# A two-block transformer kernel on one core: the norms' reciprocal square root as a power on GpSimd, and large SBUF buffers at steps of 1,024 bytes

## What is computed

```python
def rmsnorm(x, g):
    return x * lax.rsqrt(jnp.mean(x * x, axis=-1, keepdims=True) + EPS) * g    # EPS = 1e-6

def first_block(x, c, ctx, c_ctx, ...):
    h  = modulate(rmsnorm(x, norm1_g), sh1, sc1)         # norm 1: 512 tokens
    hc = modulate(rmsnorm(ctx, norm1_g), csh1, csc1)     # norm 2: 256 context tokens
    x = x + g1 * merge_branches(neighborhood_attention(...), spatial_gating(...), ...) # "out"
    h2 = modulate(rmsnorm(x, norm2_g), sh2, sc2)         # norm 3
    x = x + g2 * peer_ffn(h2, ...)      # 16,384 experts, computed densely: U, gates, then V
    return rmsnorm(x, final_g)                           # norm 4

def second_block(x, ...):
    proj = rms_norm(x, norm_mix) @ w_in                  # norm 5
    x = x + (sigmoid(ga) * (att @ w_att_o) + sigmoid(gr) * (ret @ w_ret_o)) @ w_out
    h = rms_norm(x, norm_ffn)                            # norm 6
    x = x + (silu(h @ w_gate) * (h @ w_up)) @ w_down
    return rms_norm(x, final_norm)                       # norm 7
```

## Time and profile before

| | |
|---|---|
| median of 3 runs | 3146.31 us |
| profiled execution | 3148.33 us, its span 3146.5 us |
| TensorE matmul busy | 2984.7 us, 95% of the span, 13,212 instructions |
| VectorE busy | 1462.3 us, 46% |
| ScalarE busy | 1080.6 us, 34% |
| GpSimd busy | 1167.5 us, 37% |
| mean granted TensorE clock | 0.969 |
| DMA | 417.05 MB, 133 GB/s on average |

### The profile page before, as it was taken

The page is one execution under the profiler, slowest core; times in us unless marked ns, Lnnn a source line. Parts: engine busy times, 40 slices in busy tenths (PEclk is TensorE's granted clock), DMA queues, the critical chain, the costliest instruction groups (busy, mean ns, idle before and its releaser), DMA issues.

```text
span 3146.5 us, 39584 instructions
## 1 busy us (share of the span) xinstructions
PE 2984.7 (95%) x13212; PEld 2372.9 (75%) x13256; DVE 1462.3 (46%) x2578; ACT 1080.6 (34%) x1740; POOL 1167.5 (37%) x494
## 2 busy tenths in 40 slices
PE   3988999899999999999999999999798899999998
PEld 2756877688888888887888888888585588778876
DVE  8266723149964555551555555555416731221101
ACT  4244333333335555553222222222313332232221
POOL 5310534335443333334444444444240054344442
PEclk7989999999999999999999999999898899999999
DMA  5310722224454545545666666666130033223321
GB/s 224 107 41 1 278 93 94 87 94 146 150 180 146 194 161 187 186 163 201 192 187 187 189 187 187 187 187 174 53 95 25 11 107 94 87 80 100 94 94 53
DMA packets 252690, 417.05 MB, mean 133 GB/s; under 512 B 149456, under 2 KB 150864, under 8 KB 250816
## 3 DMA queue, kind: packets, MB, share of 16 engines
q1 hardware_dynamic: 227440, 371.51, 37.8%
q10 hardware_dynamic: 22976, 37.23, 3.3%
q0 software_dynamic: 2192, 7.24, 1.0%
HBM read 345.93 MB, written 69.99 MB: 132 GB/s over the span
## 4 chain that ended last, share of the span: by engine, by line
PE 91%; DVE 4%; issue 2%; ACT 1%; DMA 1%; DVEq 0%; SPq 0%; ACTq 0%
PE bank L952 27%; PE bank L954 27%; PE bank L953 27%; PE bank L1168 2%; PE bank L1157 2%; PE bank L1049 1%; PE bank L993 1%; DVE T L1374 1%; PE bank L1029 1%; DVE rr L1370 1%; PE bank L1041 1%; PE bank L1286 1%; PE bank L1268 0%; DMA act_dram<-actb 0%; PE bank L1122 0%
## 5 line engine op out<-in xcount | busy, mean ns | idle before, releaser
L500 POOL TENSOR_TENSOR wlo<-wraw,whi 128x1024 fp32r<-128x1024 f32 x456 | 1122.6, 2463 | 1753.9 <-ACT whi L580 1753.7
L952 PE MATMUL bank<-HH,whi 128*128 128x512 f32 x2160 | 872.7, 404 | 77.2 <-DVE HL L1385 50.4
L954 PE MATMUL bank<-HH,wlo 128*128 128x512 f32 x2160 | 845.5, 391 | 0.0
L953 PE MATMUL bank<-HL,whi 128*128 128x512 f32 x2160 | 844.3, 391 | 0.0
L580 ACT ACTIVATE whi<-wraw 128x1024 fp32r<-128x1024 f32 x456 | 482.1, 1057 | 951.7 <-PE bank L954 855.0
L952 PEld LDWEIGHTS bank<-HH,whi 128*128 128x128 f32 x2160 | 408.5, 189 | 177.8 <-issue 75.6
L1683 DVE TENSOR_TENSOR WL<-AJ,WH 128x512 fp32r<-128x512 f32 x128 | 315.0, 2461 | 352.9 <-ACT WH L823 352.9
L954 PEld LDWEIGHTS bank<-HH,wlo 128*128 128x128 f32 x2160 | 407.8, 189 | 87.5
L953 PEld LDWEIGHTS bank<-HL,whi 128*128 128x128 f32 x2160 | 408.7, 189 | 84.1 <-issue 0.2
L952 PE MATMUL bank<-WH,whi 128*128 128x512 f32 x1024 | 405.8, 396 | 2.8 <-DVE WL L1683 2.8
L953 PE MATMUL bank<-WL,whi 128*128 128x512 f32 x1024 | 405.6, 396 | 0.0
(11 more groups left out here) (259 smaller groups left out, 3046.2 us busy)
## 6 DMA issues: line engine op xcount, KB each, us to landing
wraw<-in_w SPq DMA_DIRECT2D x456, 512.0 KB, 3.6
act_dram<-actb ACTq DMA_DIRECT2D x128, 256.0 KB, 2.9
gate_dram<-GS SPq DMA_DIRECT2D x8, 4096.0 KB, 13.0
AJ<-act_dram SPq DMA_DIRECT2D x128, 256.0 KB, 2.8
GJ<-gate_dram SPq DMA_DIRECT2D x128, 256.0 KB, 3.8
adaw<-in_ada SPq DMA_DIRECT2D x32, 512.0 KB, 5.4
ada<-in_ada SPq DMA_DIRECT2D x16, 512.0 KB, 14.2
E<-in_rpb POOLq DMA_DIRECT2D x16, 224.0 KB, 4.9
```

The source lines that it names most:

```text
L500: nc.gpsimd.tensor_tensor(wlo[:, slot, :, :].rearrange("p k c -> p (k c)"), wraw[:, slot, :, :].rearrange("p k c -> p (k c)"), whi[:, slot ...
L952: pe.matmul(out_, ah, bh, start=first, stop=False, **kw)
L953: pe.matmul(out_, ah, bl, start=False, stop=False, **kw)
L954: return pe.matmul(out_, al, bh, start=False, stop=last, **kw)
```

## The change

1. Each norm's square root on ScalarE (`norm_root`) goes, and so does VectorE's reciprocal. VectorE adds EPS to the sum while it copies it out of PSUM into `rms` (signal `n_var`), GpSimd raises it to the power -1/2 into `rstd` (signal `n_root`), and VectorE goes on. GpSimd's seven powers are put between its weight subtractions: the first behind its eight context products, the second behind the low parts of tiles 0 to 2, the others where the next tile waits for that norm anyway.
2. The matrix of ones becomes a matrix of 1/D (`mean`), so that the sum is a mean; the group norm's constants take the factor back.
3. The small tiles are allocated first, and tiles of 2,048 bytes or more start on a multiple of 1,024. `wraw` then starts at byte 23,552 and the phase buffers at 138,240.

```diff
@@ -104,10 +105,26 @@
-            return lambda name, shape, dt=F32: stack.enter_context(nc.sbuf_tensor(name, shape, dt))
+            def tile(name, shape, dt=F32):
+
+                big = 4 * math.prod(shape[1:]) >= 2048
+                return stack.enter_context(nc.sbuf_tensor(name, shape, dt, align_bytes=1024 if big else 32))
+            return tile
         sb = allocator(ctx)
+        cols = sb("cols", [P, NCOL])
+        mod = sb("mod", [P, 48, 2])
+        gsc = sb("gsc", [P, 3, KB])
+        ident = sb("ident", [P, P])
+        mean = sb("mean", [P, P])
+        iota = sb("iota", [P, P])
+        eps = sb("eps", [P, 2])
+        st = sb("st", [P, 24])
+        bn = sb("bn", [P, TB, 6])
+        rr = sb("rr", [P, 2, S])
+        rms, rstd = rr[:, 0, :], rr[:, 1, :]
+        sc_row = rr[:, :, :].rearrange("p a b -> p (a b)")
@@ -115,18 +132,6 @@
-        cols = sb("cols", [P, NCOL])
-        mod = sb("mod", [P, 48, 2])
-        gsc = sb("gsc", [P, 3, KB])
-        ident = sb("ident", [P, P])
-        ones = sb("ones", [P, P])
-        iota = sb("iota", [P, P])
-        eps = sb("eps", [P, 1])
-        rr = sb("rr", [P, 2, S])
-        rms, rstd = rr[:, 0, :], rr[:, 1, :]
-        sc_row = rr[:, :, :].rearrange("p a b -> p (a b)")
-        st = sb("st", [P, 24])
-        bn = sb("bn", [P, TB, 6])
@@ -294,6 +299,7 @@
+        n_var = sem("n_var")
@@ -384,7 +390,7 @@
-            for dst, src in ((X[:, :, :], A["x"]), (cols[:, :], A["cols"]), (ones[:, :], A["ones"])):
+            for dst, src in ((X[:, :, :], A["x"]), (cols[:, :], A["cols"]), (mean[:, :], A["mean"])):
@@ -516,10 +522,21 @@
+            pool.wait_ge(n_eps, 2)
+            norms = [0]
+
+            def norm_rstd(width):
+
+                norms[0] += 1
+                pool.wait_ge(n_var, norms[0])
+                nc.gpsimd.tensor_tensor(rstd[:, 0:width], rms[:, 0:width], bc(eps[:, 1:2], 1, width)[:, :, 0], ALU.pow).then_inc(n_root, 1)
...
+            norm_rstd(S)
@@ -533,7 +550,9 @@
-            los(0, 6)
+            los(0, 3)
+            norm_rstd(CTX)
+            los(3, 3)
@@ -555,9 +574,14 @@
+            norm_rstd(S)
...
-            los(G0["wq"] + 3, G0["rg"] - G0["wq"])
+            los(G0["wq"] + 3, G0["aq"] - G0["wq"])
+            norm_rstd(S)
+            norm_rstd(S)
+            los(G0["aq"] + 3, G0["rg"] - G0["aq"])
@@ -565,7 +589,10 @@
-            los(G0["rg"] + 3, NT - G0["rg"] - 3)
+            los(G0["rg"] + 3, G0["gateup"] - G0["rg"])
+            norm_rstd(S)
+            los(G0["gateup"] + 3, NT - G0["gateup"] - 3)
+            norm_rstd(S)
@@ -592,7 +619,6 @@
-            norms = [0]
@@ -604,12 +630,6 @@
-            def norm_root(width, b=4):
-                norms[0] += 1
-                act.wait_ge(n_sum, norms[0])
-                nc.scalar.activation(rms[:, 0:width], bank[b][:, 0:width], ACT.Sqrt, bias=eps[:, 0:1], scale=1.0 / D)\
-                    .then_inc(n_root, 1)
@@ -623,8 +643,6 @@
-            act.wait_ge(n_eps, 1)
-            norm_root(S)
@@ -637,7 +655,6 @@
-            norm_root(CTX)
@@ -832,12 +848,10 @@
-            norm_root(S, 0)
...
-            norm_root(S)
@@ -884,7 +898,7 @@
-                nc.scalar.activation(rst4[:, h, :], bank[4 + h][:, :], ACT.Sqrt, bias=eps[:, 0:1], scale=1.0 / 256)\
+                nc.scalar.activation(rst4[:, h, :], bank[4 + h][:, :], ACT.Sqrt, bias=eps[:, 0:1], scale=D / 256)\
@@ -990,7 +1002,7 @@
-                    mm = pe.matmul(bank[b][:, 0:width], ones[:, :], T[:, kb, 0:width], start=(kb == 0),
+                    mm = pe.matmul(bank[b][:, 0:width], mean[:, :], T[:, kb, 0:width], start=(kb == 0),
@@ -1305,12 +1317,12 @@
-                    mm = pe.matmul(bank[4 + h][:, :], ones[:, :], OT[:, 2 * h + vb, :], start=(vb == 0), stop=(vb == 1))
+                    mm = pe.matmul(bank[4 + h][:, :], mean[:, :], OT[:, 2 * h + vb, :], start=(vb == 0), stop=(vb == 1))
...
-                    mm = pe.matmul(bank[4 + h][:, :], ones[:, :], T[:, 2 * h + vb, :], start=(vb == 0), stop=(vb == 1))
+                    mm = pe.matmul(bank[4 + h][:, :], mean[:, :], T[:, 2 * h + vb, :], start=(vb == 0), stop=(vb == 1))
@@ -1364,10 +1376,12 @@
-            def norm_rstd(width):
+            def norm_rstd(width, b=4):
+
                 scaled[0] += 1
+                v.wait_ge(n_sum, scaled[0])
+                nc.vector.tensor_scalar(rms[:, 0:width], bank[b][:, 0:width], EPS, None, ALU.add).then_inc(n_var, 1)
                 v.wait_ge(n_root, scaled[0])
-                then(nc.vector.reciprocal(rstd[:, 0:width], rms[:, 0:width]))
@@ -1402,7 +1416,8 @@
-            nc.vector.memset(eps[:, :], EPS).then_inc(n_eps, 1)
+            for k, value in enumerate((EPS, -0.5)):
+                nc.vector.memset(eps[:, k:k + 1], value).then_inc(n_eps, 1)
@@ -1694,7 +1709,7 @@
-            norm_rstd(S)
+            norm_rstd(S, 0)
@@ -1793,7 +1808,7 @@
-                    nc.vector.scalar_tensor_tensor(o, bank[4 + h][:, :], -1.0 / 256, o, ALU.mult, ALU.add)\
+                    nc.vector.scalar_tensor_tensor(o, bank[4 + h][:, :], -D / 256, o, ALU.mult, ALU.add)\
@@ -1962,7 +1977,7 @@
-        cols=np.concatenate([tables[n] for n in COLS], 1), ones=np.ones((P, P), f), ident=np.eye(P, dtype=f),
+        cols=np.concatenate([tables[n] for n in COLS], 1), mean=np.full((P, P), 1.0 / D, f), ident=np.eye(P, dtype=f),
```

More of the change, by code:

```diff
@@ L12 @@
+import math
 from contextlib import ExitStack
```

## The result

The kernel after takes **3642.7 us** (median of 4 runs, 3641.1 to 3643.8) against 3146.65 for the kernel before beside it (4 runs, 3143.7 to 3150.9). The ratio is 1.1575, 95% interval 1.1555 to 1.1595: slower by 15.8%, where a gain of 0.7% was forecast. The profiled execution has a span of 3639.3 us, 492.8 more than before.

A forecast was written before the change was run, and what follows sets the result against it. TensorE was taken to bound the kernel, with 91% of the chain. Terms -27.3 + 1.1 + 4 = -22.2 us took the profiled 3148.33 to 3126.1, hence 3124 as median; range 3095 to 3165.

The forecast's parts named there:

- Part 1: Matmul streams from phase buffers: starting at multiples of 1,024 bytes, 4,080 matmuls gain 6.7 ns each, 27.3 us.
- Part 2: Five norms on the chain: addition, hops and power replace 4.13 us each, costing 1.1 us more in total.
- p: Length of one GpSimd power of 512 columns, taken as 3.35 us, between 1.2 and 5.9.
- Part 3: First norm and context's norm at the start: powers and shifted GpSimd subtractions delay the first K tile, taken as +4 us.
- Part 4: Folded 1/D, ScalarE's removed wait, extra memset and regrouped GpSimd loops: no effect on the time.
- The slope: Each microsecond of the power's length costs 5 on the chain's five norms plus 1.5 at the start.
- Rival A: Slow power between VectorE's addition and first scaling makes the kernel slower; above 6.8 us a loss, at 10 us 3167; chance 0.18.
- B: Start address is not what slows the phase-buffer streams: 0 instead of -27.3, 3151 us; chance 0.14.
- C: All matmul streams get faster, `HH` too: -145 instead of -27, 3006 us; chance 0.12.
- D: As forecast: power between 1.2 and 5.9 us, slow streams at `HH`'s rate, 3110 to 3141 us; chance 0.53.

The follow-up runs named there:

- residues_b: The kernel before with the new allocation alone, but the weight ring moved 832 bytes past a multiple of 1,024; 3180.46 us in one run.
- product_for_power: The kernel after with a GpSimd multiplication by 1e-6 in place of the power, all waits kept; 3114.34 us, ratio 0.99.

## Why the prediction was wrong

**Part 1, buffers: right in size, wrong in its reason.** -27.3 was forecast; 26 us came with the allocation alone, 28 between the two kernels with the power. `WH` went to 884, `RH` to 42.8 us, `HH` stayed. But the text took the start's own place past 1,024 as the cause. It is the distance to the weights: 704 bytes (192 modulo 256) for the phase buffers of the kernel before and 0 for `HH`. A reading of the same rows was at hand, since `whi` too was known to start 128 past, like `HH`; the prediction compared each buffer with 1,024 and not with the other operand. That this cost nothing is luck: putting all on multiples happens to set all distances to 0. By the prediction's reason, `residues_b` should have kept both streams fast.

**Part 2, the five norms: the step that failed.** The term was p, taken as 3.35 us, with bounds of 1.2 and 5.9. It measured 81.9. Everything around it held: addition 0.70, hops 0.1 together, place on the chain. The clock stayed below full after it as well (granted 0.76 from 767.9 to 774.9 us, against 0.59 from 563.5 to 570.5 before). The upper bound was no bound. It was made by carrying the price of VectorE's reciprocal against its copy over to GpSimd's subtraction, and neither is a power. No row of before showed an operation of that kind on that engine. The prediction said so ("No row has a power") and then still set the range as if the nearest rows enclosed it.

GpSimd's product takes 1.04 to 1.26 us where VectorE's subtraction of the same shape takes 0.68, 1.5 to 1.8 times as long. The Trainium skill (GPSIMD Engine Reference, section 4.1 Engine selection) gives about 2 times for two-input elementwise work; the product comes near that. It doesn't price a power, which takes 120 times as long here (81.9 against 0.68 us).

**Part 3, the start: the second step that failed, of some 5 us.** The first norm went as written. "+0.7 + p" was forecast for its scalings; they begin 82.6 us later with the power (137.61 against 54.98) and 1.85 with the product (p = 1.05). The context's norm did not. The prediction's own sum, 80.6 + 1.5p + 2.4 (or 6.9) + 5.4, gives 90.0 to 94.5 with the product's p, that is -1.1 to +3.4, and +5.2 was measured; with p = 81.9 it gives +120.2 to +124.7, and +126.8 was measured. The measured +5.2 lies inside the "+2.3 to +6.8" of the text only by chance, since those are the values for p = 3.35. What ended last was not the subtraction for tile 3, as the text had it, but the context's scalings, three of which ran beside the three subtractions and took 6.4 us more. The prediction counted exactly this collision for the row products of the first norm, and left it out for the second.

**Part 4, at nothing:** no run tests its items singly; they are right as far as the sum closes, within 1 us.

**The slope and the rivals.** "Every microsecond of p costs 5 + 1.5" gives -22.2 + 6.5 x 78.55 = +488, or 3635 us, against 3642.7 measured. Between the product (p = 1.05) and the power (81.9) the runs show 528.4 us for 80.9 of p, 6.53 per microsecond. So the model of the kernel was right within some 8 us of 496, and one price in it was wrong by a factor of 24. Rival A named the mechanism, the place and the point from which it decides, 6.8 us, but thought of 10 us and got 0.18. Rivals B and C fall: the streams did change, and `HH` stayed at 884. D held for the streams and failed by p.

**Open.** Why a power costs 160 ns a column wasn't looked into beyond the five pairs of values, 16 and 128 partitions, and the places of its tile that were tried. Whether the distances between the table's entries follow it, and what in the chip makes the distance count, wasn't tried. `wraw`, `whi` and `wlo` moved together in every run, so the distance to the weights that TensorE loads isn't told apart from the distance to the tiles that ScalarE and GpSimd work on meanwhile. A power on another engine wasn't tried either.

## What to carry to other kernels

An operation that the trace of before doesn't show, on an engine that it doesn't show it on, has no upper bound from its neighbours: leave the range open on that side, or measure the operation alone before it goes on the chain five times. Where two streams of equal matmuls run at different rates, look at where the moving tile starts relative to the weights' tile; here, putting a few small tiles in front of the large ones is worth 0.8%. Two changes put into one can hide a good one: the allocation alone gains 26 us, the two together lose 496.

## What the runs showed of the hardware

- GpSimd's power of float32 tiles took 160 ns per column and 0.3 us, whether the exponent was -0.5, 1 or 2 and whether 16 or 128 partitions were used (81.9 to 82.2 us for 512 columns); a product of the same shape took 1.04 to 1.26 us.
- TensorE's distance between matmuls of 512 fp32r columns, each with its own weight load, went with the start of the moving tile relative to the weights' tile in SBUF: 226.2 to 227.2 ns at a multiple of 256, 229 at 64, 232 to 234 at 32, 96, 128, 192 and 224 (modulo 256); 0, 64, 128 and 192 in two or more places of the weights, the others in one.
- A scaling of 256 columns on VectorE took 2.59 to 2.62 us beside a GpSimd subtraction and 0.47 without one (`product_for_power`).
- The hops VectorE to GpSimd and back took 0.07 and 0.03 us on the chain, with a semaphore each (`product_for_power`; 0.07 and 0.02 with the power).
